# Stick-breaking attention: turns and scores of two neighbouring units alternate, their value products run in one burst

## Chip, cores and metric

The kernel runs on one core of a Trainium2 chip. The metric is the device time of one execution in microseconds (us). The kernel before took 3842.76 us, the median of 3 runs (3842.71 to 3846.33).

## What is computed

One layer of a streaming encoder: a root-mean-square norm with a modulation, one input projection, two groups of heads side by side (an mLSTM with a matrix memory, and stick-breaking attention), and one output projection with a norm and a residual. The change lies in the stick-breaking attention alone (8 heads of 64, 4096 tokens):

```
z        = einsum('bthd,bshd->bhts', q, k)              # scaled by d**-0.5
strict   = s < t
log_keep = where(strict, log_sigmoid(-z), 0)
after    = cumsum(log_keep, reverse over s) - log_keep
A        = where(strict, exp(log_sigmoid(z) + after), 0)
out      = einsum('bhts,bshd->bthd', A, v)
```

The kernel works with keep = sigmoid(-z) and its running product from the right. The product of a position less that of its left neighbour is A, so with differences of neighbouring v rows (the tile `dw`) the products themselves can be multiplied with the values, and a row of v is added at the end (`v_e`).

## The kernel before

There are five stages one after the other: modulation, norm, input projection, attention (`stage_attend`), and a last stage with the mLSTM recurrence and the output projection (`stage_mix`). A stage begins when the one before is through.

`stage_attend` cuts its work into **units**. A unit is a pair of heads (4 pairs), a block `cb` of 256 queries (16, from the last to the first) and a block `j` of 512 keys, from the diagonal leftwards. All units of one query block make a **row**; a row has `cb // 2 + 1` units: 8, 8, 7, 7, 6, 6, 5, 5, 4, 4, 3, 3, 2, 2, 1, 1. That is 72 for a pair of heads and 288 in all. The first unit of a row lies on the diagonal and is narrower (`width`, `blocks`, `skip`): for an odd `cb` its scores are 384 and 512 keys wide, for an even one 128 and 256.

A unit u goes through these steps:

- **scores(u)**, TensorE, L916: 12 matmuls, two heads side by side on the two 64-row halves of the array. They fill the four score banks `z` (ZB = 4, one unit's worth). After the third part of each half, `z_done` rises.
- **gates(u)**, ScalarE, L973: four sigmoids, from `z` to `keep` (KB = 8 slots, two units).
- masks, GpSimd, L876: on diagonal units only.
- **scans(u)**, VectorE, L1057: four running products, from `keep` to `prod` (PB = 3 units). Each starts from the result of the unit to its right.
- **turn(u)**, TensorE, L927: 16 transposes (14 or 6 on the diagonal), in four blocks of keys, into three rotating banks `rt` (RB = 3). The fourth block needs a bank back, so it waits until the first block was copied (`turned_done`).
- **copies(u)**, ScalarE, L982: one copy per block, from `rt` to `turned` (TB = 8 slots, two units).
- **weigh(u)**, TensorE, L938: the value products, on 64-column halves of the array, summed over the row in the single bank `acc`. The program's 8 matmuls of a unit stand as 16 records in the trace.
- **row_out(u)**, ScalarE, L992: two moves of `acc` to `osum` after a row's last unit. The next row's first value product waits for them (`row_done`).

The order on each engine is written out by hand. TensorE runs, for every u:

```
turn(u)
if u + 2 < NU:
    scores(u + 2)
if u:
    weigh(u - 1)
```

ScalarE runs `row_out(u - 2)`, `copies(u)`, `gates(u + 2)`. VectorE runs the scans in the order of the units. SyncE loads keys and queries ahead and stores each row. GpSimd, beside its masks, splits the output weights for the last stage.

Of the kernel before, what the change touches and what calls it, by code (L numbers as in the profile page):

```python
# [8 lines left out]
ACT = mybir.ActivationFunctionType  # L9

P = 128
# [11 lines left out]
Z_SCALE = float(SD) ** -0.5  # L23
# [706 lines left out]
def stage_attend(nc, d, cols, wout_hi, wout_lo, w_out):  # L730
    NP = SH // 2
    QW = 2 * P
    UNITS, LAST = [], {}
# [6 lines left out]
    NU = len(UNITS)  # L740
    ZB, RB = 4, 3
    KB, PB, TB = 8, 3, 8
# [4 lines left out]
    def width(u, i):  # L747
        return (UNITS[u][2] % 2 * 2 + i + 1) * P if diag(u) else CH

    def blocks(u):  # L750
        return UNITS[u][2] % 2 * 2 + 2 if diag(u) else TPC

    def skip(u, kb):
        return max(0, kb - UNITS[u][2] % 2 * 2) if diag(u) else 0

    FIRST, OWNER = [], []
# [2 lines left out]
        OWNER += [u] * blocks(u)  # L759
    FIRST.append(len(OWNER))  # L760

    with ExitStack() as ctx:
        sb = lambda n, s, dt=F32: ctx.enter_context(nc.sbuf_tensor("a_" + n, s, dt))
        ps = lambda n, s, dt=F32: ctx.enter_context(nc.psum_tensor("a_" + n, s, dt))
# [4 lines left out]
        keep = sb("keep", [P, KB, CH])  # L769
        prod = sb("prod", [P, PB, 4, CH])  # L770
        turned = sb("turned", [P, TB, CH])
# [10 lines left out]
        z = [ps(f"z{k}", [P, CH]) for k in range(ZB)]  # L782
        rt = [ps(f"rt{k}", [P, CH]) for k in range(RB)]
# [5 lines left out]
        z_done, keep_done, mask_done, scan_done = sem("z_done"), sem("keep_done"), sem("mask_done"), sem("scan_done")  # L789
# [6 lines left out]
        def after(eng, semaphore, value):  # L796

            if value > 0:
                eng.wait_ge(semaphore, value)
# [80 lines left out]
        @block.tensor  # L880
        def _(pe):
            pe.wait_ge(const, 3)
            pe.wait_ge(v_in, 16)
            for hp in range(NP):
                last = pe.transpose(rt[2][:, P + hp * NT:P + (hp + 1) * NT], vrow[:, hp * P:(hp + 1) * P], ident[0:NT, 0:NT])
            last.then_inc(ve_tr, 1)

            pe.wait_ge(g_dve, 4)
            pe.transpose(z[0][0:1, 0:P], b[:, P - 1:P], ident[:])
            pe.transpose(z[0][0:1, P:2 * P], top[:, P - 1:P], ident[:]).then_inc(g_pe, 1)  # L890
            pe.transpose(rt[0][:, 0:P], u_g[:], ident[:])
            pe.transpose(z[3][:, 0:P], b[:], ident[:]).then_inc(g_pe, 1)

            pe.wait_ge(g_dve, 11)
            row = lambda t: t[:].rearrange("a h c -> a (h c)")
            pe.matmul(z[1][:, 2 * P:2 * P + 1], row(mprev_row), ones[0:1, 0:1], start=True, stop=True)
            pe.matmul(z[1][:, 0:P], ones[0:1, :], row(mprev_row), start=True, stop=True)
            pe.matmul(z[1][:, P:2 * P], ones[0:1, :], row(mlast_row), start=True, stop=True).then_inc(g_pe, 1)
            pe.wait_ge(g_dve, 14)
            pe.transpose(rt[1][:, 0:P], m[:], ident[:]).then_inc(g_pe, 1)  # L900
            pe.wait_ge(g_dve, 20)
            pe.wait_ge(ve_done, 1)

            def scores(u):
                hp, row, cb, j = UNITS[u]
                g = row // 2
                pe.wait_ge(q_in[g % 2], 32 * (g // 2 + 1))
                pe.wait_ge(chunk_in[j], 64 * (hp + 1))
                for i in range(2):
                    at, w = 4 * u + 2 * i, width(u, i)  # L910
                    after(pe, keep_done, at + 2 - ZB)
                    t, s = (cb % 2 * 2 + i) * P, slice(j * CH, j * CH + w)
                    for part, (qp, k) in enumerate(((0, khi), (1, khi), (0, klo))):
                        for h in range(2):
                            e = slice(h * SD, (h + 1) * SD)
                            mm = pe.matmul(z[(at + h) % ZB][:, 0:w], q_sb[e, g % 2, qp, t:t + P], k[e, s], start=part == 0, stop=part == 2)  # L916
                            if part == 2:
                                mm.then_inc(z_done, 1)

            def turn(u):  # L920
                pe.wait_ge(scan_done, 4 * u + 4)
                for kb in range(blocks(u)):
                    k = FIRST[u] + kb
                    after(pe, turned_done, k + 1 - RB)
                    for h in range(2):
                        for i in range(skip(u, kb), 2):
                            last = pe.transpose(rt[k % RB][:, h * QW + i * P:h * QW + (i + 1) * P], prod[:, u % PB, 2 * i + h, kb * P:(kb + 1) * P], ident[:])  # L927
                    last.then_inc(rt_done, 1)

            def weigh(u):  # L930
                _, row, cb, j = UNITS[u]
                if diag(u):
                    after(pe, row_done, row)
                pe.wait_ge(turned_done, FIRST[u + 1])
                for kb in range(blocks(u)):
                    for h in range(2):
                        lo = skip(u, kb) * P
                        last = pe.matmul(acc[h * SD:(h + 1) * SD, lo:], dw[:, h, j * TPC + kb, :], turned[:, (FIRST[u] + kb) % TB, h * QW + lo:(h + 1) * QW],  # L938
                                         start=diag(u) and kb == 0, stop=j == 0 and kb == blocks(u) - 1, skip_group_check=True)
                last.then_inc(av_done, 1)  # L940

            scores(0)
            scores(1)
            for u in range(NU):
                turn(u)
                if u + 2 < NU:
                    scores(u + 2)
                if u:
                    weigh(u - 1)
            weigh(NU - 1)  # L950

        @block.scalar
        def _(act):
            act.preload_act_table_set("natural_log_exp_and_others")
            act.wait_ge(g_in, 32)
            act.activation(soft[:], fg[:], ACT.Abs).then_inc(g_act, 1)
            act.wait_ge(g_act, 1)
            act.activation(soft[:], soft[:], ACT.Exp, scale=-1.0).then_inc(g_act, 1)
            act.wait_ge(g_act, 2)
            act.activation(soft[:], soft[:], ACT.Ln, bias=1.0).then_inc(g_act, 1)  # L960
            act.wait_ge(ve_tr, 1)
            act.copy(v_e[:], rt[2][:, P:P + NP * NT]).then_inc(ve_done, 1)
            act.wait_ge(g_dve, 20)
            act.activation(cols["wk"][:], xw[:], ACT.Exp).then_inc(g_act, 1)
            act.activation(cols["decay"][:], xs[:], ACT.Exp).then_inc(g_act, 1)
            act.activation(cols["floor"][:], xe[:], ACT.Exp, scale=-1.0).then_inc(g_act, 1)

            def gates(u):
                for s in range(4):
                    at, w = 4 * u + s, width(u, s // 2)  # L970
                    act.wait_ge(z_done, at + 1)
                    after(act, scan_done, at + 1 - KB)
                    act.activation(keep[:, at % KB, 0:w], z[at % ZB][:, 0:w], ACT.Sigmoid, scale=-Z_SCALE).then_inc(keep_done, 1)  # L973

            def copies(u):
                for kb in range(blocks(u)):
                    k, lo = FIRST[u] + kb, skip(u, kb) * P
                    act.wait_ge(rt_done, k + 1)
                    if k >= TB:
                        act.wait_ge(av_done, OWNER[k - TB] + 1)  # L980
                    by_head = lambda t: t.rearrange("p (h q) -> p h q", h=2)[:, :, lo:] if lo else t
                    act.copy(by_head(turned[:, k % TB]), by_head(rt[k % RB][:])).then_inc(turned_done, 1)  # L982

            def row_out(u):
                hp, row, cb, _ = UNITS[u]
                if LAST[row] != u:
                    return
                act.wait_ge(av_done, u + 1)
                after(act, o_st[row % 2], 16 * (row // 2))
                for i in range(2):  # L990
                    at = hp * NT + 2 * cb + i
                    out = act.activation(osum[:, row % 2, i * P:(i + 1) * P], acc[:, i * P:(i + 1) * P], ACT.Identity, bias=v_e[:, at:at + 1])  # L992
                out.then_inc(row_done, 1)

            gates(0)
            gates(1)
            for u in range(NU):
                if u >= 2:
                    row_out(u - 2)
                copies(u)  # L1000
                if u + 2 < NU:
                    gates(u + 2)
            row_out(NU - 2)
            row_out(NU - 1)

        @block.vector
# [461 lines left out]
```

## Time and profile before

| | |
|---|---|
| median of 3 runs | 3842.76 us |
| the profiled execution's own time | 3846.45 us |
| its span, first to last instruction | 3843.9 us |
| mean granted TensorE clock, of full speed | 0.976 |
| TensorE matmul busy | 3676.7 us, 96% |
| VectorE busy | 2325.4 us, 60% |
| ScalarE busy | 1825.4 us, 47% |

The profile page gives shares over the whole span. The attention units run from about 1852.7 to 3301 us of it, and what the change does has to be read in that stretch. A row of the timeline merges neighbouring instructions of one line and shape: start, length of the group, count, and in brackets the idle time ahead of it with what ended it. The groups of matmuls of two stages overlap in it, because matmuls are pipelined: the time that a stage takes is the distance between starts. The change adds lines: L916, L927 and L938 of the kernel before are L924, L935 and L946 after it, L973 and L982 are L979 and L987, L992 is L997.

### The profile page before, as it was taken

Reading aid. Unit: us, or ns where it says so; the run is one execution under the profiler, and the core shown is the slowest. Engines: PE = TensorE matmul, PEld = TensorE weight load, DVE = VectorE, ACT = ScalarE, POOL = GpSimd, SP = SyncE. Lnnn points to the kernel's source line nnn. Section 1 sums busy time; section 2 is a strip of 40 time slices with the busy share of each in tenths; the row PEclk is TensorE's granted clock in tenths of the full one; section 3 lists DMA queues with packets and bytes.
Section 4 is the critical chain, followed back from the end, with each engine's and each line's share of the span. In section 5 each row is a group of like instructions: output and inputs, shape, how many; then the busy total and the mean of one; then the engine's idle time right before and its main releaser. Section 6 shows DMA issues by size and latency. Waiting matters only on the chain. (4 is left out here: it accounts for less than half of the span.)

```text
span 3843.9 us, 63586 instructions
## 1 busy us (share of the span) xinstructions
PE 3676.7 (96%) x22351; PEld 2846.6 (74%) x22351; DVE 2325.4 (60%) x3224; ACT 1825.4 (47%) x3782; POOL 568.4 (15%) x591
## 2 busy tenths in 40 slices
PE   6399999999999999999799999999999999799998
PEld 2388878887888788877577777777777777588887
DVE  2578882223222211223788898888888888566665
ACT  2423331112211211212577777787777777455554
POOL 0211210001332232000000100010001000233332
PEclk8699999999999999999899999999999999899999
DMA  7743232225555444233300210120012000466664
GB/s 267 282 170 115 93 134 93 90 105 180 184 179 184 159 137 147 91 118 114 110 25 27 62 40 27 38 74 18 22 42 66 10 18 28 122 199 199 202 202 138
DMA packets 258950, 433.76 MB, mean 113 GB/s; under 512 B 27812, under 2 KB 151076, under 8 KB 252295
## 3 DMA queue, kind: packets, MB, share of 16 engines
q1 hardware_dynamic: 248952, 403.98, 31.0%
q0 software_dynamic: 9808, 27.28, 2.5%
q8 instruction: 115, 1.88, 0.2%
q14 instruction: 75, 0.61, 0.0%
HBM read 288.37 MB, written 147.00 MB: 113 GB/s over the span
## 5 line engine op out<-in xcount | busy, mean ns | idle before, releaser
L1057 DVE TENSOR_TENSOR_SCAN a_prod<-a_keep,a_prod,a_zeros 128x512 f32<-128x512 f32 x896 | 1072.3, 1264 | 102.0 <-ACT a_keep L973 100.8
L982 ACT COPY a_turned<-a_rt 128x512 f32<-128x512 f32 x1088 | 548.1, 590 | 234.1 <-PE a_rt L927 233.8
L973 ACT ACTIVATE a_keep<-a_z 128x512 f32<-128x512 f32 (+3 forms) x1152 | 556.6, 575 | 40.1 <-PE a_z L916 39.8
L510 PE MATMUL p_bank<-p_hhi,p_whi 128*128 128x512 f32 (+1 forms) x1344 | 524.7, 390 | 35.4 <-DVE p_hlo L633 30.0
L927 PEld LDWEIGHTS a_rt<-a_ident,a_prod 128*128 128x128 f32 x4224 | 451.6, 140 | 113.5 <-issue 66.1
L927 PE MATMUL a_rt<-a_ident,a_prod 128*128 128x128 f32 x4224 | 531.1, 278 | 4.1 <-DVE a_prod L1057 3.3
L510 PE MATMUL p_bank<-p_hlo,p_whi 128*128 128x512 f32 (+1 forms) x1344 | 524.0, 390 | 0.0
L510 PE MATMUL p_bank<-p_hhi,p_wlo 128*128 128x512 f32 (+1 forms) x1344 | 524.0, 390 | 0.0
L938 PE MATMUL a_acc<-a_turned,a_dw 128*64 128x256 f32 x4352 | 519.6, 379 | 0.7 <-ACT a_osum L992 0.7
L938 PEld LDWEIGHTS a_acc<-a_turned,a_dw 128*64 128x64 f32 x4352 | 286.7, 136 | 212.7 <-issue 91.7
L510 PE MATMUL p_bank<-p_whi,p_hhi 128*128 128x512 f32 x1024 | 401.0, 392 | 11.7 <-DVE p_wlo L643 11.6
L510 PE MATMUL p_bank<-p_whi,p_hlo 128*128 128x512 f32 x1024 | 400.2, 391 | 0.0
L510 PE MATMUL p_bank<-p_wlo,p_hhi 128*128 128x512 f32 x1024 | 400.1, 391 | 0.0
L916 PE MATMUL a_z<-a_khi,a_q 64*128 64x512 f32 (+3 forms) x2304 | 372.5, 402 | 1.3 <-DVE a_xe L1043 0.9
L510 PEld LDWEIGHTS p_bank<-p_hhi,p_whi 128*128 128x128 f32 (+1 forms) x1344 | 246.6, 183 | 97.1 <-issue 37.7
L510 PEld LDWEIGHTS p_bank<-p_hhi,p_wlo 128*128 128x128 f32 (+1 forms) x1344 | 246.6, 183 | 58.9
L510 PEld LDWEIGHTS p_bank<-p_hlo,p_whi 128*128 128x128 f32 (+1 forms) x1344 | 246.6, 183 | 58.7
L1057 DVE TENSOR_TENSOR_SCAN a_prod<-a_keep,a_zeros 128x384 f32<-128x384 f32 (+3 forms) x256 | 220.1, 918 | 49.7 <-POOL a_keep L876 49.7
L876 POOL TENSOR_SCALAR_AFFINE_SELECT a_keep<-a_keep 128x256 f32<-128x256 f32 x128 | 68.1, 535 | 1196.9 <-ACT a_keep L973 1193.8
L916 PEld LDWEIGHTS a_z<-a_khi,a_q 64*128 64x128 f32 x2304 | 192.4, 185 | 70.4 <-issue 49.1
L712 DVE TENSOR_TENSOR p_hlo<-p_hraw,p_hhi 128x4096 fp32r<-128x4096 f32 x32 | 142.1, 4441 | 167.3 <-ACT p_hhi L588 167.3
L510 PEld LDWEIGHTS p_bank<-p_whi,p_hhi 128*128 128x128 f32 x1024 | 193.3, 189 | 54.9 <-issue 12.8
(197 smaller groups left out, 4386.1 us busy)
## 6 DMA issues: line engine op xcount, KB each, us to landing
p_hraw<-scratch_hT SPq DMA_DIRECT2D x42, 2048.0 KB, 7.8
n_xt<-in_x SPq DMA_DIRECT2D x8, 2048.0 KB, 11.1
scratch_hT<-n_hout SPq DMA_DIRECT2D x8, 2048.0 KB, 7.5
m_xt<-in_x SPq DMA_DIRECT2D x32, 512.0 KB, 4.8
out_y<-m_ot SPq DMA_DIRECT2D x32, 512.0 KB, 3.1
n_wada<-in_w_ada SPq DMA_DIRECT2D x4, 2048.0 KB, 15.2
scratch_mlq<-p_oa SPq DMA_DIRECT2D x32, 256.0 KB, 2.3
scratch_mlk<-p_oa SPq DMA_DIRECT2D x32, 256.0 KB, 2.4
```

Source lines behind the costliest of these rows:

```text
L510: last = pe.matmul(dst, stationary, moving, start=(k == 0 and q == 0), stop=(k == KT - 1 and q == 2))
L712: dve.tensor_tensor(hlo[:, 1 - p], hraw[:], hhi[:, 1 - p].bitcast(F32), ALU.subtract).then_inc(h_lo, 1)
L876: pool.affine_select(out=tail, in_=tail, compare_op=ALU.is_gt, fill=1.0, base=0, pattern=[[0, 2], [-1, P]], channel_multiplier=1).then_inc ...
L916: mm = pe.matmul(z[(at + h) % ZB][:, 0:w], q_sb[e, g % 2, qp, t:t + P], k[e, s], start=part == 0, stop=part == 2)
L927: last = pe.transpose(rt[k % RB][:, h * QW + i * P:h * QW + (i + 1) * P], prod[:, u % PB, 2 * i + h, kb * P:(kb + 1) * P], ident[:])
L938: last = pe.matmul(acc[h * SD:(h + 1) * SD, lo:], dw[:, h, j * TPC + kb, :], turned[:, (FIRST[u] + kb) % TB, h * QW + lo:(h + 1) * QW], st ...
L973: act.activation(keep[:, at % KB, 0:w], z[at % ZB][:, 0:w], ACT.Sigmoid, scale=-Z_SCALE).then_inc(keep_done, 1)
L982: act.copy(by_head(turned[:, k % TB]), by_head(rt[k % RB][:])).then_inc(turned_done, 1)
L1057: dve.tensor_tensor_scan(prod[:, u % PB, s, 0:w][:, ::-1], keep[:, at % KB, 0:w][:, ::-1], zeros[:, 0:w], first, ALU.mult, ALU.add).then_i ...
```

## The change

Units of a row are counted from its diagonal (`step_of`). An even unit and the odd one behind it make a pair; `burst(u)` says which value products follow turn(u) and scores(u + 2): none after the pair's first unit, both after its second, and the unit's own where it is a row's last and without a partner. Each pair of heads has 32 pairs and 8 such single units. On ScalarE the copies of a pair's second unit are put among the gates of the unit behind it: three gates, two copies, the fourth gate, two copies. `row_out` now comes right after the burst that ends a row.

```diff
+    def step_of(u):
+        return u - (LAST[UNITS[u][1] - 1] + 1 if UNITS[u][1] else 0)
+
+    def burst(u):
+        if step_of(u) % 2 == 1:
+            return [u - 1, u]
+        return [u] if LAST[UNITS[u][1]] == u else []
...
                 turn(u)
                 if u + 2 < NU:
                     scores(u + 2)
-                if u:
-                    weigh(u - 1)
-            weigh(NU - 1)
+                for done in burst(u):
+                    weigh(done)
...
-            gates(0)
-            gates(1)
+            for u in range(2):
+                for k in range(4):
+                    gate(u, k)
             for u in range(NU):
-                if u >= 2:
-                    row_out(u - 2)
-                copies(u)
-                if u + 2 < NU:
-                    gates(u + 2)
-            row_out(NU - 2)
+                if u >= 1 and burst(u - 1):
+                    row_out(u - 1)
+                first = not burst(u)
+                merged = step_of(u) % 2 == 1
+                if not merged:
+                    for kb in range(blocks(u)):
+                        copy(u, kb)
+                if first:
+                    for kb in range(max(4, blocks(u + 1))):
+                        if u + 2 < NU and kb == 0:
+                            for k in range(3):
+                                gate(u + 2, k)
+                        if u + 2 < NU and kb == 2:
+                            gate(u + 2, 3)
+                        if kb < blocks(u + 1):
+                            copy(u + 1, kb)
+                elif u + 2 < NU:
+                    for k in range(4):
+                        gate(u + 2, k)
             row_out(NU - 1)
```

`gate` and `copy` do for one slot or block what `gates` and `copies` did for a unit, with the same waits.

TensorE in the middle of a row, before (a_rt are turns, a_z scores, a_acc value products):

```order
L927 MATMUL a_rt<-a_ident,a_prod 128x128 x16
L916 MATMUL a_z<-a_khi,a_q 128x512 x4
L916 MATMUL a_z<-a_klo,a_q 128x512 x2
L916 MATMUL a_z<-a_khi,a_q 128x512 x4
L916 MATMUL a_z<-a_klo,a_q 128x512 x2
L938 MATMUL a_acc<-a_turned,a_dw 64x256 x8
L927 MATMUL a_rt<-a_ident,a_prod 128x128 x16
L916 MATMUL a_z<-a_khi,a_q 128x512 x4
L916 MATMUL a_z<-a_klo,a_q 128x512 x2
L916 MATMUL a_z<-a_khi,a_q 128x512 x4
L916 MATMUL a_z<-a_klo,a_q 128x512 x2
L938 MATMUL a_acc<-a_turned,a_dw 64x256 x8
```

and now:

```order
L935 MATMUL a_rt<-a_ident,a_prod 128x128 x16
L924 MATMUL a_z<-a_khi,a_q 128x512 x4
L924 MATMUL a_z<-a_klo,a_q 128x512 x2
L924 MATMUL a_z<-a_khi,a_q 128x512 x4
L924 MATMUL a_z<-a_klo,a_q 128x512 x2
L935 MATMUL a_rt<-a_ident,a_prod 128x128 x16
L924 MATMUL a_z<-a_khi,a_q 128x512 x4
L924 MATMUL a_z<-a_klo,a_q 128x512 x2
L924 MATMUL a_z<-a_khi,a_q 128x512 x4
L924 MATMUL a_z<-a_klo,a_q 128x512 x2
L946 MATMUL a_acc<-a_turned,a_dw 64x256 x16
L935 MATMUL a_rt<-a_ident,a_prod 128x128 x16
```

Two turns with their scores now come with no value product between them, and the value products of both units follow as one group of 16.

ScalarE at the same place, before (a_turned are copies, a_keep gates):

```order
L982 COPY a_turned<-a_rt 128x512 x4
L973 ACTIVATE a_keep<-a_z 128x512 x4
L982 COPY a_turned<-a_rt 128x512 x4
L973 ACTIVATE a_keep<-a_z 128x512 x4
L982 COPY a_turned<-a_rt 128x512 x4
```

and now:

```order
L987 COPY a_turned<-a_rt 128x512 x4
L979 ACTIVATE a_keep<-a_z 128x512 x3
L987 COPY a_turned<-a_rt 128x512 x2
L979 ACTIVATE a_keep<-a_z 128x512
L987 COPY a_turned<-a_rt 128x512 x2
L979 ACTIVATE a_keep<-a_z 128x512 x4
L987 COPY a_turned<-a_rt 128x512 x4
```

Three of four gates now stand ahead of the first copy of every second unit.

TensorE where a row of an odd number of units ends and one with an even query block begins (the turn of 6 is the narrow diagonal unit), before:

```order
L916 MATMUL a_z<-a_khi,a_q 128x512 x4
L916 MATMUL a_z<-a_klo,a_q 128x512 x2
L916 MATMUL a_z<-a_khi,a_q 128x512 x4
L916 MATMUL a_z<-a_klo,a_q 128x512 x2
L938 MATMUL a_acc<-a_turned,a_dw 64x256 x8
L927 MATMUL a_rt<-a_ident,a_prod 128x128 x6
L916 MATMUL a_z<-a_khi,a_q 128x512 x4
L916 MATMUL a_z<-a_klo,a_q 128x512 x2
L916 MATMUL a_z<-a_khi,a_q 128x512 x4
L916 MATMUL a_z<-a_klo,a_q 128x512 x2
L938 MATMUL a_acc<-a_turned,a_dw 64x256 x8
L927 MATMUL a_rt<-a_ident,a_prod 128x128 x16
```

and now:

```order
L924 MATMUL a_z<-a_khi,a_q 128x512 x4
L924 MATMUL a_z<-a_klo,a_q 128x512 x2
L924 MATMUL a_z<-a_khi,a_q 128x512 x4
L924 MATMUL a_z<-a_klo,a_q 128x512 x2
L946 MATMUL a_acc<-a_turned,a_dw 64x256 x8
L935 MATMUL a_rt<-a_ident,a_prod 128x128 x6
L924 MATMUL a_z<-a_khi,a_q 128x512 x4
L924 MATMUL a_z<-a_klo,a_q 128x512 x2
L924 MATMUL a_z<-a_khi,a_q 128x512 x4
L924 MATMUL a_z<-a_klo,a_q 128x512 x2
L935 MATMUL a_rt<-a_ident,a_prod 128x128 x16
```

Between the scores ahead and the turn of 16 behind there were two groups of value products, and now there is one.

## Rows read from the trace of the kernel before

**Rows 1.** Page, part 1: busy time, share of the span, instructions of each engine.
```profile
PE 3676.7 (96%) x22351; PEld 2846.6 (74%) x22351; DVE 2325.4 (60%) x3224; ACT 1825.4 (47%) x3782; POOL 568.4 (15%) x591
```

**Rows 2.** Windows: all attention units, then one steady pair (us; busy of each engine; clock; DMA).
```profile
1852.70:3301.00 1448.30, 1442.98 (x12032) 1031.39 (x12032) 1291.64 (x1152) 1137.65 (x2371) 122.50 (x192) 1.00 0.12 37
2602.00:2612.77 10.77, 10.77 (x90) 7.64 (x89) 9.62 (x9) 8.26 (x16) 0.00 (x0) 1.00 0.01 2
```

**Rows 3.** Waits in attention: who waited on what, us in total, times, longest us.
```profile
PEld a_acc L938 <- issue: 91.7, 254, 0.4
```

**Rows 4.** Timeline, TensorE, one steady unit: start, us, engine, line, tiles, shapes, count.
```profile
2607.07 0.39 PE L938 MATMUL a_acc<-a_turned,a_dw 128*64 128x256 f32 x2
2607.38 1.99 PE L927 MATMUL a_rt<-a_ident,a_prod 128*128 128x128 f32 x16
2609.30 0.73 PE L916 MATMUL a_z<-a_khi,a_q 64*128 64x512 f32 x4
2609.87 0.39 PE L916 MATMUL a_z<-a_klo,a_q 64*128 64x512 f32 x2
2610.10 0.62 PE L916 MATMUL a_z<-a_khi,a_q 64*128 64x512 f32 x4
2610.57 0.40 PE L916 MATMUL a_z<-a_klo,a_q 64*128 64x512 f32 x2
2610.89 1.95 PE L938 MATMUL a_acc<-a_turned,a_dw 128*64 128x256 f32 x16
2612.77 0.44 PE L927 MATMUL a_rt<-a_ident,a_prod 128*128 128x128 f32 x2
```

**Rows 5.** Timeline, TensorE, the same unit without each first transpose and first product pair.
```profile
2607.55 1.72 PE L927 MATMUL a_rt<-a_ident,a_prod 128*128 128x128 f32 x14
2611.16 1.68 PE L938 MATMUL a_acc<-a_turned,a_dw 128*64 128x256 f32 x14
```

**Rows 6.** Timeline, ScalarE, the same unit: copies, then gates, with the wait before.
```profile
2608.08 2.06 ACT L982 COPY a_turned<-a_rt 128x512 f32<-128x512 f32 x4 [1.10 <-PE a_rt L927]
2610.30 2.07 ACT L973 ACTIVATE a_keep<-a_z 128x512 f32<-128x512 f32 x4 [0.16 <-PE a_z L916]
```

**Rows 7.** Timeline, VectorE, the scans that belong to the scores at 2609.30.
```profile
2610.93 4.81 DVE L1057 TENSOR_TENSOR_SCAN a_prod<-a_keep,a_prod,a_zeros 128x512 f32<-128x512 f32 x4 [0.57 <-ACT a_keep L973]
```

**Rows 8.** Timelines, TensorE then ScalarE: a turn whose first copy comes late.
```profile
2585.67 1.53 PE L927 MATMUL a_rt<-a_ident,a_prod 128*128 128x128 f32 x12
2587.39 0.66 PE L927 MATMUL a_rt<-a_ident,a_prod 128*128 128x128 f32 x4 [0.19 <-ACT a_turned L982]
2587.97 0.73 PE L916 MATMUL a_z<-a_khi,a_q 64*128 64x512 f32 x4
...
2586.71 2.10 ACT L982 COPY a_turned<-a_rt 128x512 f32<-128x512 f32 x4
2588.97 1.09 ACT L973 ACTIVATE a_keep<-a_z 128x512 f32<-128x512 f32 x2 [0.16 <-PE a_z L916]
```

**Rows 9.** Timelines, TensorE then VectorE: unit 24, second of an even block's row.
```profile
1975.93 0.73 PE L916 MATMUL a_z<-a_khi,a_q 64*128 64x512 f32 x4
...
1983.66 1.99 PE L927 MATMUL a_rt<-a_ident,a_prod 128*128 128x128 f32 x16
...
1977.56 13.29 DVE L1057 TENSOR_TENSOR_SCAN a_prod<-a_keep,a_prod,a_zeros 128x512 f32<-128x512 f32 x11 [1.99 <-ACT a_keep L973]
```

**Rows 10.** Timelines, TensorE then VectorE: units 139 and 145, around a change of heads.
```profile
2551.57 0.74 PE L916 MATMUL a_z<-a_khi,a_q 64*128 64x512 f32 x4
...
2559.51 1.99 PE L927 MATMUL a_rt<-a_ident,a_prod 128*128 128x128 f32 x16
...
2574.22 0.62 PE L916 MATMUL a_z<-a_khi,a_q 64*128 64x384 f32 x4
...
2580.64 11.84 DVE L1057 TENSOR_TENSOR_SCAN a_prod<-a_keep,a_prod,a_zeros 128x512 f32<-128x512 f32 x10
```

**Rows 11.** Timeline, TensorE: the last product of the stage.
```profile
3300.06 0.87 PE L938 MATMUL a_acc<-a_turned,a_dw 128*64 128x256 f32 x8 [0.73 <-ACT a_osum L992]
```

More of the change, by code:

```diff
@@ L966, in _, with gate, copy @@
             act.activation(cols["floor"][:], xe[:], ACT.Exp, scale=-1.0).then_inc(g_act, 1)
[L968 to L982, printed above, removed]
+            def gate(u, s):
+                at, w = 4 * u + s, width(u, s // 2)
+                act.wait_ge(z_done, at + 1)
+                after(act, scan_done, at + 1 - KB)
+                act.activation(keep[:, at % KB, 0:w], z[at % ZB][:, 0:w], ACT.Sigmoid, scale=-Z_SCALE).then_inc(keep_done, 1)
+            def copy(u, kb):
+                k, lo = FIRST[u] + kb, skip(u, kb) * P
+                act.wait_ge(rt_done, k + 1)
+                if k >= TB:
+                    act.wait_ge(av_done, OWNER[k - TB] + 1)
+                by_head = lambda t: t.rearrange("p (h q) -> p h q", h=2)[:, :, lo:] if lo else t
+                act.copy(by_head(turned[:, k % TB]), by_head(rt[k % RB][:])).then_inc(turned_done, 1)
             def row_out(u):
```

## The prediction

> **What bounds the kernel now.** The page's busy times come first [rows 1]: TensorE is busy for 96% of the span, VectorE for 60%, ScalarE for 47%. These are averages over five stages, so I went on to the table by stretch for attention alone [rows 2]. There TensorE shows a matmul in flight for 1443 of 1448 us, at a granted clock of 1.00 (2.4 GHz), VectorE is busy for 1292 us (89%) and ScalarE for 1138 us (79%). One matmul or another is always in flight, so nothing can be gained by filling holes; what counts is the distance between starts of one stage and the next, and the timeline gives it. In the steady state a turn starts at 2607.38, the scores at 2609.30, the products at 2610.89, the next turn at 2612.77 [rows 4]: 1.92 + 1.59 + 1.88 = 5.39 us a unit. All of the change lies on TensorE's own path, so what it saves or adds there is time of the kernel, as long as the engines behind it keep up.
>
> How near are they? **ScalarE**: its four gates begin 1.00 us behind the scores, its four copies 0.70 us behind the turn, and each four take 2.07 us with about 0.48 us from one start to the next [rows 6]. **VectorE**: its first scan begins 1.63 us behind the scores and the four take 4.81 us [rows 7]. So a unit's turn can start at the earliest 6.44 us behind its scores, and with some 0.05 us for the semaphore I take 6.49. Before, the path between them is two units less a turn, 8.85 us; 2.4 us are to spare.
>
> **Part 1: fewer switches.** TensorE goes through three kinds of work, and each switch costs something the starts show. Leaving: the last product pair stands 0.31 us ahead of the turn (2607.07 to 2607.38), where pairs inside the group stand 0.217 apart (14 records span 1.68) [rows 4, 5]; the last score pair stands 0.32 ahead of the products (2610.57 to 2610.89), inside it is 0.23 [rows 4]. Either exit costs 0.095. Entering: the second transpose comes 0.165 behind the first, the others at 0.11, so 0.055; the second product pair comes 0.27 behind the first, so 0.05 [rows 4, 5]. A pair of units had six switches and now has five: product to turn and scores to product go once, scores to turn comes new. Net, one exit and one entry into products go away: 0.095 + 0.05 = **0.145 us a pair**. A switch from scores to turn stands nowhere in steady state; I take it as the exit from scores plus the entry to turns, 0.15. Its bounds are nothing and 0.20, the dearest one seen (turn to scores: 0.09 out and 0.10 in, from the distances of rows 4), which makes -19 and +6 us of the total; 0.15 is nearest, since exits cost the same whatever follows. For 4 x 32 = 128 pairs: -18.6 us.
>
> A second reading of a switch is larger. The weight loads stand idle for 0.36 us ahead of a product group, 91.7 us over 254 times [rows 3]. The Trainium skill ("Perfetto Trace Analysis", Identifying the Most-Contended Engine) holds that matmul busy time is a poor measure and that the share of weight loads is a good one; by [rows 2] that share is 1031 of 1448 us, 71%, and by this rule a switch is worth the whole idle of the loads and not 0.145. By that, 128 x 0.36 = 46 us would go. I go by the starts, since the matmuls close up to 0.095 across that same idle.
>
> **Part 2: the copy that comes late.** The fourth block of a turn takes the bank that the first copy frees. In steady state this is just in time: 0.70 us behind the turn. Where that copy came late before, the trace shows the price [rows 8]: the turn of 2585.67 had its first copy at 2586.71, 1.04 us behind, its last four transposes waited until 2587.39, 0.68 us after the copy, and the turn took 2.30 us instead of 1.92. So 0.35 us late cost 0.38, which is the lateness and 0.03 more. Now take a pair's second turn. It starts 1.59 us behind the scores of the unit after it. Those scores' first gate starts at 1.00, and three gates go ahead of the copy: 1.00 + 3 x 0.48 = 2.44 with rounding. The copy thus starts 0.85 us behind its turn and not 0.70, 0.16 late, and the turn gets **0.19 us** longer. This eats more than the saving. It holds for pairs followed by a full unit. Where the next unit is the narrow one of a new row (8 rows of 16, those of an even number of units) its gates are shorter and the copy comes in time, and four pairs wait for VectorE anyway (part 3). That leaves 32 - 8 - 4 = 20 pairs for each pair of heads: 80 x 0.19 = +15.0 us. Bounds are nothing (the gates end sooner) and 0.38 (as late as in rows 8): 0 to 30 us. The rest of ScalarE's queue has room: the fourth gate starts 1.8 us behind the second turn, while the score half that needs its bank starts 2.9 behind it; the last copy is done by 3.4 and the unit's products start at 3.7. The gates of the next unit start some 0.13 us later than before, hidden by VectorE, which is still on the scans before. Row sums wait as before: they stand behind the row's last product and ahead of the copies, also now. SyncE's and GpSimd's queues keep their order; their triggers shift by less than a unit, and DMA is busy for 12% [rows 2].
>
> **Part 3: turns that come too early for the scans.** Within full pairs the path from scores to their turn is 12.2 us for two units of scans, 1.63 + 9.62 + 0.05 = 11.3: no wait. Around narrow units it is tight. Where a narrow unit of an even query block opens a row behind a single unit, moving the products takes one group of 1.88 us out of the path. That is so three times for each pair of heads, at the turns of units 24, 48 and 64: the scores of unit 24 start at 1975.93, its turn at 1983.66, 7.73 later [rows 9]. Less 1.88 that is 5.85, but the scans need 6.49 (VectorE starts at 1977.56 there and goes on without a hole [rows 9]): a wait of 0.64. Unit 139, in a short row near a change of heads, has 7.94 - 1.88 = 6.06 [rows 10] and waits 0.43. Unit 145, behind the change, has 2574.22 to 2585.67 = 11.45, less 1.88 = 9.57; its scans are four from 2580.64 on, at 11.84 / 10 each, done by 2585.43, and with the semaphore this is 11.26 behind those scores [rows 8, 10]: 1.69, less the 0.38 that its late copy cost before, 1.31. Sum: 4 x (3 x 0.64 + 0.43) + 3 x 1.31 = 9.4 + 3.9 = +13.3 us. Bounds: nothing, if scans start sooner, and twice as much, if the masks on GpSimd get late too.
>
> **Part 4: the end.** The last two units are single, with no scores left to cover their copies, so each of the last two product groups waits about 1 us for its own copies (the fourth starts 0.70 + 3 x 0.48 = 2.1 us behind its turn and takes 0.5 or more, while a turn of 14 is through after 1.7); before, the last group waited 0.73 us for the row sum [rows 11]. I take +1.1 us.
>
> **Sum**: -18.6 + 15.0 + 13.3 + 1.1 = +10.8 us. The profiled execution took 3846.45 us by its own time (span 3843.9), 3.7 above the median of 3842.76; it would take 3857.3, and the median **3853.6 us**.
>
> **The rivals.**
>
> - *The late copy doesn't hold the turn.* That needs the three gates to end 0.16 us sooner, or a bank that comes free otherwise. For it: 0.16 is a small difference of large numbers. Against it: the wait of rows 8 follows the copy to the hundredth. 3853.6 - 15.0 = 3838.6, no difference that shows.
> - *Faster: a switch is worth more than the starts say.* Its place is each burst, where the second product group needs no new start of the weight loads; its price the 0.36 us of [rows 3], 46 us in all. Against waits of 29.4 us this gives 3842.8 - 46 + 29 = 3826. It decides from 0.29 us a pair on. For it: the loads do idle there. Against it: 0.095 + 0.05 is all that the matmuls' starts lose. The rule of the Trainium skill named above would have it so.
> - *Slower than I say: the waits compound.* If the second turn's copy comes as late as in rows 8, each costs 0.38: another 15 us, 3869.
> - *It does nothing that shows*, saving and waits cancel out: about 3843.
>
> **How the numbers follow.** 0.2% (7.7 us) is about what a measurement of this kernel can tell from no change: same is 3835.1 to 3850.4. Forecast 0.56 (of which 0.04 below 3850.4, by a cheaper scores-to-turn switch), late copy harmless 0.14 (0.01 of it faster), dear switches 0.12, compounding 0.10, nothing 0.08. Faster 0.13, same 0.25, slower 0.62. The range leaves out the faster rival and half of the compounding one: 3836 to 3867.
>
> **What would show it.** Right: L935 takes 1.92 us for the first turn of a pair and 2.11 for the second, split at its twelfth transpose with "ACT a_turned" as the releaser; waits of L935 on "DVE a_prod" of 0.6 us three times a pair of heads; 16 + 16 product records without a step at the middle; scores to second turn 1.59 us. Wrong: second turns of 1.92 us (part 2 falls), no waits on VectorE (part 3 falls), or a switch from scores to turn far from 0.15 (part 1). A granted clock under 1.00 in attention would break the frame of all of it, and I expect no single wait above 1.7 us.

## The result, and the profile after

The changed kernel takes 3856.09 us, the median of 7 runs (3853.51 to 3859.63), against 3842.99 us for the kernel before, the median of 7 runs beside it (3840.93 to 3846.33). The ratio is 1.0032 with a 95% interval of 1.0021 to 1.0044: slower by 8 to 17 us. 3853.6 was predicted, in a range of 3836 to 3867.

The profiled execution took 3853.51 us, with a span of 3851.3. From the page, part 1, the counterpart of [rows 1]:

```profile
PE 3673.1 (95%) x22351; PEld 2854.1 (74%) x22351; DVE 2318.5 (60%) x3224; ACT 1801.6 (47%) x3782; POOL 564.3 (15%) x591
```

These shares say nothing: TensorE is busy for less time in a slower kernel. The table by stretch, for attention from its first score to its last product, answers to [rows 2]:

```profile
1849.70:3309.40 1459.70, 1441.95 (x12032) 1041.52 (x12032) 1284.71 (x1152) 1115.85 (x2370) 121.61 (x192) 1.00 0.12 37
```

1459.7 us where it was 1448.3, with TensorE's granted clock at 1.00 as before. **Attention is 11.4 us longer**; 10.8 were predicted. The rest of this profile's span went the other way by 4 us: attention began at 1849.7 and not at 1852.7, and what follows its last product took 541.9 us and not 542.9. These parts are the same program in both kernels. Over all the profiled executions of this study the start of attention lies between 1847.9 and 1853.4 us, so I read every experiment first by its attention stretch, which doesn't carry that scatter, and then by the medians. A stretch comes from one profiled execution of each kernel, and how far it scatters itself was not measured; the differences of stretches and of medians below agree to about 3 us.

The timeline of TensorE in a steady pair, the counterpart of [rows 4]:

```profile
2606.66 1.99 PE L935 MATMUL a_rt<-a_ident,a_prod 128*128 128x128 f32 x16
2608.57 0.73 PE L924 MATMUL a_z<-a_khi,a_q 64*128 64x512 f32 x4
...
2609.84 0.40 PE L924 MATMUL a_z<-a_klo,a_q 64*128 64x512 f32 x2
2610.16 2.17 PE L935 MATMUL a_rt<-a_ident,a_prod 128*128 128x128 f32 x16
2612.27 0.73 PE L924 MATMUL a_z<-a_khi,a_q 64*128 64x512 f32 x4
...
2613.85 3.67 PE L946 MATMUL a_acc<-a_turned,a_dw 128*64 128x256 f32 x32
2617.46 0.33 PE L935 MATMUL a_rt<-a_ident,a_prod 128*128 128x128 f32 x1
```

The pair's first turn takes 1.91 us, its scores up to the second turn 1.59, the second turn 2.11, its scores 1.58 and the 32 product records in one group 3.61: 10.80 us, where two units took 10.77 before. The switch from scores to turn, which no row of before showed, costs the same as the others: 2609.84 to 2610.16 is 0.32 from the last score pair, as it was ahead of products.

The weight loads of the second turn, and ScalarE beside them (copies, three gates, two copies, the fourth gate), which answer to [rows 8, 6]:

```profile
2610.16 1.29 PEld L935 LDWEIGHTS a_rt<-a_ident,a_prod 128*128 128x128 f32 x12 [0.36 <-issue]
2611.68 0.42 PEld L935 LDWEIGHTS a_rt<-a_ident,a_prod 128*128 128x128 f32 x4 [0.22 <-ACT a_turned L987]
```

```profile
2607.35 2.06 ACT L987 COPY a_turned<-a_rt 128x512 f32<-128x512 f32 x4 [2.60 <-PE a_rt L935]
2609.57 1.58 ACT L979 ACTIVATE a_keep<-a_z 128x512 f32<-128x512 f32 x3 [0.17 <-PE a_z L924]
2611.02 1.10 ACT L987 COPY a_turned<-a_rt 128x512 f32<-128x512 f32 x2
2611.96 0.66 ACT L979 ACTIVATE a_keep<-a_z 128x512 f32<-128x512 f32 x1
```

The turn starts at 2610.16, its first copy at 2611.02, 0.86 us behind; the load of the thirteenth transpose waits for that copy until 2611.68. All 80 turns that were counted in the prediction show this, with the copy 0.85 to 0.86 us behind and a length of 2.09 to 2.11 us.

Unit 24, which answers to [rows 9], first TensorE and then VectorE:

```profile
1974.81 0.73 PE L924 MATMUL a_z<-a_khi,a_q 64*128 64x512 f32 x4
...
1979.08 0.74 PE L924 MATMUL a_z<-a_khi,a_q 64*128 64x512 f32 x4
...
1981.30 1.99 PE L935 MATMUL a_rt<-a_ident,a_prod 128*128 128x128 f32 x16 [0.55 <-DVE a_prod L1076]
```

```profile
1976.43 14.22 DVE L1076 TENSOR_TENSOR_SCAN a_prod<-a_keep,a_prod,a_zeros 128x512 f32<-128x512 f32 x12 [2.56 <-ACT a_keep L979]
```

Its scores start at 1974.81, its scans 1.62 us later and without a hole; the scores ahead of its turn start at 1979.08, and the turn follows after 2.22 us and not 1.59, released by VectorE. That is 0.63 us, at 12 places of the stage. Around the change of heads, which answers to [rows 8, 10] (units 143, 144, 146, 145):

```profile
2583.20 0.87 PE L946 MATMUL a_acc<-a_turned,a_dw 128*64 128x256 f32 x8
2584.25 1.91 PE L935 MATMUL a_rt<-a_ident,a_prod 128*128 128x128 f32 x14 [0.17 <-DVE a_prod L1076]
2586.09 0.73 PE L924 MATMUL a_z<-a_khi,a_q 64*128 64x512 f32 x4
...
2588.95 1.99 PE L935 MATMUL a_rt<-a_ident,a_prod 128*128 128x128 f32 x16 [1.21 <-DVE a_prod L1076]
```

The turn of unit 145 starts 2.86 us behind the scores ahead of it and not 1.59. Last, the waits of attention in total, where 91.7 us of idle ahead of product loads stood before [rows 3], and the end of the stage:

```profile
PEld a_rt L935 <- DVE a_prod L1076: 81.2, 173, 3.2
PEld a_acc L946 <- issue: 33.2, 90, 1.1
PEld a_acc L946 <- ACT a_turned L987: 19.3, 53, 0.4
PEld a_rt L935 <- ACT a_turned L987: 18.6, 84, 0.2
```

```profile
3302.47 1.77 PE L935 MATMUL a_rt<-a_ident,a_prod 128*128 128x128 f32 x14
3305.15 1.74 PE L946 MATMUL a_acc<-a_turned,a_dw 128*64 128x256 f32 x16 [0.91 <-ACT a_turned L987]
3306.81 0.87 PE L935 MATMUL a_rt<-a_ident,a_prod 128*128 128x128 f32 x6
3308.51 0.87 PE L946 MATMUL a_acc<-a_turned,a_dw 128*64 128x256 f32 x8 [0.82 <-ACT a_turned L987]
```

Both last product groups wait for their copies, 0.91 and 0.82 us. The totals of waits above are idle time of the weight loads and not lost time: a load group ahead of a turn stands idle for about 0.39 us even where nothing is late (at 2607.38 in the kernel before it is 0.39, put down to "issue"). What is lost shows in the starts. Over the whole stage, turns come at 28 places later than their usual distance behind the scores ahead (1.59, 1.42 or 0.88 us by width), 14.4 us in all.

The longest wait of the matmuls is at the stage's first turn, 2.81 us for VectorE. That turn starts 7.9 us behind the first scores of the stage (1849.71 to 1857.60), as it did before (1852.71 to 1860.61).

### The profile page after: what moved, and what is told of

Read it like the earlier page. It is cut to its first block and busy times, and to the rows that moved or that the text cites. A ratio compares the mean times of both kernels' runs of the same rounds, so it can differ in the third digit from the quotient of the medians.

```text
span 3851.3 us, 63586 instructions
## 1 busy us (share of the span) xinstructions
PE 3673.1 (95%) x22351; PEld 2854.1 (74%) x22351; DVE 2318.5 (60%) x3224; ACT 1801.6 (47%) x3782; POOL 564.3 (15%) x591
## 3 DMA queue, kind: packets, MB, share of 16 engines
q8 instruction: 115, 1.88, 0.2%
## 5 line engine op out<-in xcount | busy, mean ns | idle before, releaser
L987 ACT COPY a_turned<-a_rt 128x512 f32<-128x512 f32 x1088 | 567.3, 601 | 238.1 <-PE a_rt L935 236.1
L979 ACT ACTIVATE a_keep<-a_z 128x512 f32<-128x512 f32 (+3 forms) x1152 | 584.6, 610 | 24.0 <-PE a_z L924 23.7
L935 PE MATMUL a_rt<-a_ident,a_prod 128*128 128x128 f32 x4224 | 546.6, 279 | 15.6 <-DVE a_prod L1076 15.2
L946 PE MATMUL a_acc<-a_turned,a_dw 128*64 128x256 f32 x4352 | 491.3, 376 | 1.7 <-ACT a_turned L987 1.7
L946 PEld LDWEIGHTS a_acc<-a_turned,a_dw 128*64 128x64 f32 x4352 | 294.6, 137 | 181.4 <-issue 33.2
L510 PE MATMUL p_bank<-p_whi,p_hhi 128*128 128x512 f32 x1024 | 400.7, 391 | 11.5 <-DVE p_wlo L643 11.4
L884 POOL TENSOR_SCALAR_AFFINE_SELECT a_keep<-a_keep 128x256 f32<-128x256 f32 x128 | 76.5, 603 | 1240.4 <-ACT a_keep L979 1240.4
```

What stands on the lines that cost most here:

```text
L510: last = pe.matmul(dst, stationary, moving, start=(k == 0 and q == 0), stop=(k == KT - 1 and q == 2))
L884: pool.affine_select(out=tail, in_=tail, compare_op=ALU.is_gt, fill=1.0, base=0, pattern=[[0, 2], [-1, P]], channel_multiplier=1).then_inc ...
```

## The experiments

Every edit is made to the changed kernel. The kernel before was measured beside each run on the same chip, and ratios are to it.

### e1_copy_third: the copy comes earlier

The loop behind `if first:` becomes one that takes the order from a string, two gates, a copy, two gates, three copies:

```diff
-                    for kb in range(max(4, blocks(u + 1))):
...
+                    g = c = 0
+                    for op in "GGCGGCCC":
+                        if op == "G":
+                            if u + 2 < NU:
+                                gate(u + 2, g)
+                            g += 1
+                        else:
+                            if c < blocks(u + 1):
+                                copy(u + 1, c)
+                            c += 1
```

> Only ScalarE's order for a pair's second unit is changed against the changed kernel: two gates, one copy, two gates, three copies, in place of three gates, two copies, one gate, two copies. Theory (the late copy holds the second turn): its first copy starts 0.70 us behind its turn and not 0.85, all 80 second turns of 2.10 us become 1.92, so attention gets shorter by 80 x 0.19 = 15 us, less one or two that are given back at waits for the scans: TensorE's attention stretch 1446 to 1448 us where it was 1459.7, the median 3841 to 3844, level with the kernel before. Waits on the scans stay. Rival (the turn was long for another reason, such as the switch from scores to turn): second turns stay at 2.10 us and the time at 3856.

The median of 11 runs is 3840.89 us, ratio 0.9991 (0.9982 to 1.0000): level with the kernel before, and by the medians 15 us under the changed one. Its attention stretch, and ScalarE and TensorE in a steady pair:

```profile
1853.40:3299.30 1445.90, 1427.09 (x12032) 1040.18 (x12032) 1284.31 (x1152) 1124.79 (x2370) 110.48 (x192) 1.00 0.13 37
```

```profile
2606.11 1.08 ACT L979 ACTIVATE a_keep<-a_z 128x512 f32<-128x512 f32 x2 [0.17 <-PE a_z L924]
2607.40 0.58 ACT L987 COPY a_turned<-a_rt 128x512 f32<-128x512 f32 x1 [0.20 <-PE a_rt L935]
```

```profile
2603.19 1.99 PE L935 MATMUL a_rt<-a_ident,a_prod 128*128 128x128 f32 x16
...
2606.70 1.99 PE L935 MATMUL a_rt<-a_ident,a_prod 128*128 128x128 f32 x16
2608.63 0.73 PE L924 MATMUL a_z<-a_khi,a_q 64*128 64x512 f32 x4
...
2610.22 3.67 PE L946 MATMUL a_acc<-a_turned,a_dw 128*64 128x256 f32 x32
2613.83 1.99 PE L935 MATMUL a_rt<-a_ident,a_prod 128*128 128x128 f32 x16
```

The copy now starts at 2607.40, 0.70 us behind the turn of 2606.70, and that turn takes 1.93 us. All 224 turns of 16 transposes in this trace last 1.92 us to within 10 ns. Attention is 13.8 us shorter than with the change, the stretch 0.1 us below what was expected and the median as well: the theory holds, the rival falls. 80 x 0.185 = 14.8 us went from the turns. About one came back, as waits for VectorE at the turns of units 11, 39 and 59 of each pair of heads, 0.07 to 0.24 us each; the 12 of 0.63 us stayed.

This run also measures the saving of the switches by itself, since nothing in its steady pairs is late. From the first turn of a pair to the next pair's, 24 steady pairs take 10.61 to 10.63 us, where 48 pairs of units of the kernel before take 10.76 to 10.78: 0.15 us a pair.

### e2_four_gates: the copy comes still later

The same loop as in e1, with another string; the change's own order would be "GGGCCGCC":

```diff
+                    for op in "GGGGCCCC":
```

> All four gates ahead of the first copy of a pair's second unit. Theory: the copy starts one gate (0.48 us) later, 1.33 us behind its turn, and the turn ends 0.68 us after the copy starts at its twelfth transpose: 2.58 us for each of the 80 turns, and the 44 or so turns that had slack lose part of it too; at least 80 x 0.48 = 38 us, about 3900. Rival (ScalarE's order does not matter, VectorE or the switches do): no change from 3856.

3901.69 us (2 runs), ratio 1.0147 (1.0129 to 1.0166). The attention stretch:

```profile
1852.00:3358.40 1506.40, 1446.49 (x12032) 1041.06 (x12032) 1287.37 (x1152) 1122.78 (x2370) 135.61 (x192) 1.00 0.12 36
```

1506.4 us, 46.7 more than with the change. A pair's second turn on TensorE, then its copies on ScalarE:

```profile
2625.84 1.53 PE L935 MATMUL a_rt<-a_ident,a_prod 128*128 128x128 f32 x12
2627.85 0.66 PE L935 MATMUL a_rt<-a_ident,a_prod 128*128 128x128 f32 x4 [0.48 <-ACT a_turned L987]
2628.44 0.73 PE L924 MATMUL a_z<-a_khi,a_q 64*128 64x512 f32 x4
```

```profile
2627.18 2.09 ACT L987 COPY a_turned<-a_rt 128x512 f32<-128x512 f32 x4
```

The copies start 1.34 us behind the turn of 2625.84; the thirteenth transpose follows 0.67 us after that, and the turn takes 2.60 us. 80 turns are like this one. 17 others take 2.31 to 2.38, 16 of them where the gates ahead are a little narrower. The 80 are 0.49 us longer than with the change, 39 us in all; the 16 were in time there and add 16 x 0.45 = 7 us. With e1 and the changed kernel this gives the turn's length over three places of the copy: 0.70, 0.85 and 1.33 us behind the turn give 1.92, 2.10 and 2.59. From the first point on it is nearly one for one: 0.15 us late costs 0.18, 0.63 late costs 0.67.

### e3_tail_pairs: two of the waits on VectorE

`burst` is read from a table of 72 digits for each pair of heads. A 1 means that all products due run after this unit's turn and scores, a 0 that those of the unit itself wait. The change's own rule would have 0101011 for units 16 to 22 and 01011 for units 42 to 46; four digits differ, ScalarE's order stays:

```diff
+    PLAN = "010101010101010101011010101011010101010101011010101101010101011011010111"
+    SPREAD, due = [], 0
+    for u in range(NU):
+        upto = u if PLAN[u % len(PLAN)] == "1" or u == NU - 1 else u - 1
+        SPREAD.append(list(range(due, upto + 1)))
+        due = max(due, upto + 1)
+
     def burst(u):
+        return SPREAD[u]
```

> ScalarE's order as in the changed kernel. In the two rows that end with a single unit ahead of an even query block (units 20 to 22 and 44 to 46 of each pair of heads) the single unit comes two units earlier and the row ends with a burst of two, so that the turn of unit 24 (48) has one more product group ahead of it. Theory: the two waits of 0.63 us for the scans go at 8 places, -5.0 us, with up to 2 us given back by the moved copies: attention 1455 to 1457 us where it was 1459.7. Rival (those waits are not caused by the path between scores and turn): the waits stay or move elsewhere, 1459.7.

3850.72 us (11 runs), ratio 1.0019 (1.0009 to 1.0028). The attention stretch:

```profile
1851.50:3306.60 1455.10, 1439.97 (x12032) 1039.55 (x12032) 1284.52 (x1152) 1115.15 (x2370) 115.09 (x192) 1.00 0.12 37
```

1455.1 us, 4.6 less than with the change. Of the 12 places where 2.22 us stood ahead of a turn in place of 1.59, 4 are left, those of unit 64: -5.0 us. The turns of units 22 and 46, which now come behind narrow scores with one group fewer on their path, wait for VectorE instead, 0.23 us at 8 places: +1.8 us, as the expectation allowed. The rest of the 4.6 is small change at several places. At units 24 and 48 one more product group between scores and turn is all that was added, so it was the length of that path that made the wait.

### e4_both: a version that beats both

ScalarE's order of e1, and another table for the 72 units of a pair of heads: pairs in the long rows, with a single product group put earlier in the rows that e3 also changed (by other digits than in e3), and single products at the change of heads and in most short rows. It has 108 bursts of two, where the change has 128. On ScalarE, the copies and row sums follow the same table.

```diff
+    PLAN = "111101010101010101001010101011010101010101001010110101010110000001000111"
```

> Both mended: ScalarE's order of e1, and a table of 72 digits says after which turn the products run (pairs in the long rows, shifted where the scans would be late, single products in the short rows). Theory: what is left is the saving of the switches, about 0.145 us for each pair, and few waits: attention 1431 to 1436 us, the median about 3827 to 3831, 0.3 to 0.4% under the kernel before. Rival (the saving of 0.145 us a pair is not there, and the loss of the change was some other cost of bursts): not under 3843.

The median of 5 runs is **3830.54 us, ratio 0.9964 (0.9950 to 0.9977)** to the kernel before. Its attention stretch:

```profile
1852.00:3283.70 1431.70, 1426.81 (x12032) 1038.69 (x12032) 1282.68 (x1152) 1124.57 (x2370) 116.30 (x192) 1.00 0.13 38
```

1431.7 us, 16.6 under the kernel before and 28.0 under the change. By the starts, turns come 1.5 us in all later than their usual distance behind the scores ahead, where e1 has 16.8 us and the change 14.4, and no turn in the middle of the stage is longer than 1.95 us. 108 x 0.145 = 15.7 us is what the switches should save, near the 16.6. The saving of the switches is there once the two waits are not.

### e5_extra_switch: one switch more

ScalarE's order is that of e1. On TensorE:

```diff
                 turn(u)
+                if len(burst(u)) == 2:
+                    weigh(u - 1)
                 if u + 2 < NU:
                     scores(u + 2)
-                for done in burst(u):
-                    weigh(done)
+                if burst(u):
+                    weigh(u)
```

> As e1_copy_third, but each burst of two is taken apart: the first unit's products come between the second turn and its scores, the second unit's behind those scores. Same work, one switch more for each of 128 pairs (an exit from products and an entry into them). Theory: a steady pair takes 10.77 us again where e1 has 10.62, 0.145 each, 18.6 us in all; the scores come one product group later, so turns near narrow units wait some 12 us more for the scans; about 30 us over e1: attention 1474 to 1478 us, the median 3869 to 3874. Rival (a switch costs the whole 0.36 us that the weight loads stand idle): a steady pair 10.98 us, 46 us and the same waits over e1, about 3899. Rival (bursts save nothing): a steady pair 10.62 us, 3853.

3870.64 us (4 runs), ratio 1.0071 (1.0054 to 1.0088). The attention stretch, and TensorE in a steady pair:

```profile
1847.90:3324.50 1476.60, 1446.41 (x12032) 1032.04 (x12032) 1290.98 (x1152) 1136.81 (x2370) 107.73 (x192) 1.00 0.12 37
```

```profile
2602.69 1.99 PE L935 MATMUL a_rt<-a_ident,a_prod 128*128 128x128 f32 x16
...
2606.19 1.99 PE L935 MATMUL a_rt<-a_ident,a_prod 128*128 128x128 f32 x16
2608.11 1.95 PE L946 MATMUL a_acc<-a_turned,a_dw 128*64 128x256 f32 x16
...
2611.58 1.95 PE L946 MATMUL a_acc<-a_turned,a_dw 128*64 128x256 f32 x16
2613.46 0.33 PE L935 MATMUL a_rt<-a_ident,a_prod 128*128 128x128 f32 x1
```

The pair takes 2602.69 to 2613.46, 10.77 us, where e1 has 10.62. Its six switches are not those of the kernel before: turn to products and products to scores are new. A turn lasts 1.92 us here whether scores or products follow, and 16 product records 1.88 whether a turn or scores follow.

The stretch is 30.7 us longer than in e1. Waits ahead of turns, by the starts, come to 28.9 us where e1 has 16.8, so 12.1 are waits for VectorE, as expected; 10 of them are the 2.22 us that stand at 28 places and not at 12. That leaves 18.6 us for 128 switches, 0.145 each, the figure of the theory, and far from the 46 of the rival.

### e6_short_rows_single: the change of heads

The pairs of the short rows (units 52 to 71) are given up; ScalarE's order is that of e1.

The table of e3 is used again, with the change's own digits up to unit 51; a 0 behind a 0 means the products of the unit before, as in the kernel before:

```diff
+    PLAN = "010101010101010101010110101011010101010101010110101100000000000000000000"
```

> As e1_copy_third, but in the short rows of each pair of heads (query blocks 7 to 0, units 52 to 71) the products run as in the kernel before, one unit behind. Theory: the waits for the scans around the change of heads (units 64, 67, 72, 73 of each pair of heads, 0.4 to 1.4 us each) go or shrink, about 11 us, and the saving of the switches in these rows goes too, 8 pairs x 4 x 0.145 = 4.6 us (12.1 us of waits in the replay of part 3's sums), so 6 to 8 us under e1: attention 1438 to 1441 us, the median 3833 to 3836. Rival (the waits at the change of heads come from the loads of keys or queries and not from the order of the products): they stay, and the time is 4 to 5 us over e1.

3837.79 us (10 runs), ratio 0.9978 (0.9968 to 0.9987). The attention stretch:

```profile
1853.20:3292.90 1439.70, 1431.37 (x12032) 1039.20 (x12032) 1285.50 (x1152) 1127.04 (x2370) 121.29 (x192) 1.00 0.13 37
```

1439.7 us, 6.2 less than e1: more waits go than switches are given back. The waits at the turns of units 59, 64 and 67 (0.24, 0.64 and 0.44 us, four times each) and of the second unit behind each change of heads (1.3 us, three times) are gone, 9.2 us; the 8 at units 24 and 48 stay. The late copy of the kernel before [rows 8] is back three times. The loads of keys and queries are in the same places in both kernels, so they didn't make those waits. The stretch is as expected, the median is not: 3837.79 us lies above the 3833 to 3836 that were expected, and only 3.1 us below that of e1, which was measured on another chip. By the ratios, each to the kernel before beside it, it is 5 us.

## Why the prediction was right

- **The frame.** TensorE's path set the time, and the distances between starts gave it. The attention stretch came out at +11.4 us where the sum said +10.8. Against the medians (+13.1 us) the miss is 2.3 us, inside the interval of the ratio. That the sum is so near is in part luck. Taken group by group over all 288 units, the waits came to +31.0 us where 29.4 were said, and what is left for the switches is -19.6 us where -18.6 was said: two small misses that cancel.
- **Part 1, -18.6 us.** 0.145 us a pair was read from the kernel before. e1, where no copy is late, has 10.62 a pair against 10.77, and e5, which puts one switch back, is at 10.77 again. The price taken for the unseen switch from scores to turn (0.15) came out: scores last 1.59 us whether products or a turn follow.
- **Part 2, +15.0 us.** The copy was to start 0.85 us behind and the turn to take 0.19 longer, 80 times. It was 0.85 to 0.86, 0.17 to 0.19, and 80 times; e1 takes it away and e2 makes it 0.67. The turn that came late once per change of heads in the old trace already showed this price.
- **Part 3, +13.3 us.** 0.64 us at 12 places was 0.63; 0.43 us at unit 139 was 0.44 (1.32 us from its scores ahead, where 0.88 is the length); 1.31 us at the change of heads was 1.27 + 0.25 + 0.13 - 0.38 = 1.27. The prediction put all of it at the turn of unit 145, and only 1.27 of the wait stands there. The turn of unit 144 starts 0.25 us late for VectorE (2583.20 to 2584.25 is 1.05, where 8 product records take 0.80) and lasts 0.13 us longer, its first copy coming behind the row sum on ScalarE. The total holds all the same, because both pieces lie ahead of the turn of unit 145 and shorten its wait for the same scans. e3 and e6 show that the order of the products makes these waits.
- **Part 4, +1.1 us.** Two waits of 0.91 and 0.82 where one of 0.73 had been: +1.0.
- **What it left out.** Behind narrow scores the products now come before their unit's last copy is through. The loads wait 19.3 us in total for it, mostly in time that was idle anyway: such scores last 0.95 us and not 0.88, 16 times. The turns of units 59 and 69 come 0.07 us late, 8 times. Together this is 1.7 us, about what the waits came to above the prediction. The prediction also expected no single wait above 1.7 us. One of 2.81 us stands ahead of the stage's first turn; one of 1.95 us stood there in the kernel before, so its own trace already spoke against that bound, and the turn comes no later behind the stage's first scores than it did.
- **The rivals.** *Late copy harmless* is out (e1, e2). *Slower by compounding* is out: the copies kept their distance. *It does nothing that shows* is out too, since the interval of the ratio lies above 1. *A switch is worth the idle of the weight loads* is out: the idle ahead of product loads fell from 91.7 us to 33.2 + 19.3, by 39 us, while the pairs got 19 us shorter, and e5 prices the switch directly. So the weight loads' share of busy time, which the Trainium skill ("Perfetto Trace Analysis", Identifying the Most-Contended Engine) puts above matmul busy time for judging headroom, was no measure of what was to be won here: it is 71% before and 73% in e4, and neither it nor the matmuls' busy share tells how far the starts can close up.

## What to carry to other kernels

Where an engine is always busy, read its path by the distances between starts, and price a regrouping by the exit and the entry that it saves. Then walk the same stretch on the engines that feed it: a strict queue that gets one more instruction ahead of the one that frees a buffer gives the delay straight to the bound engine, and a group moved out from between a producer's start and its consumer takes the slack away from that pair. The saving here was real and both losses could be mended, once each was found at its place.

## What the runs showed that was not expected

The price of a switch on TensorE does not depend on what follows. The prediction assumed this for one switch, and all three kinds of work bear it out: from the last score pair it is 0.32 us to products and to a turn alike, 0.095 over the pitch inside the group, and e5 shows the same for turns and for products. And the dependence of a turn on its copy has no slack: 0.70, 0.85, 1.33 us give 1.92, 2.10, 2.59 us. In a turn of 1.92 us the thirteenth transpose starts 1.37 us behind the first. In e2 it starts 0.67 us behind the first copy's start. With the copy 0.70 us behind the turn these are the same 1.37 us, so that copy is just in time, and a shift of 0.15 us already shows.
